# Narrow high passes in the hidden tiles, a reordered LRU and hybrid mixer, an earlier last split in the gated blocks, and the normed activations moved by 64 bytes

## Time and profile before

| | us |
|---|---|
| median of 3 runs (lowest, highest) | 2010.35 (2008.78, 2012.93) |
| the profiled execution, own time | 2012.28 |
| its span | 2010.5 |
| PE busy in the span | 1961.8 (98%) |
| DVE busy | 1373.3 (68%) |
| ACT busy | 916.8 (46%) |

### The profile page before, as it was taken

One profiled execution on the slowest core, in us unless ns is written; L12 is line 12 of the kernel. 1 busy time (PEld: TensorE's weight loads), 2 busy tenths in 40 slices (PEclk: granted clock), 3 DMA queues, 4 the chain that ended last, 5 costly groups with the idle time before them and its releaser, 6 DMA issues.

```text
span 2010.5 us, 27811 instructions
## 1 busy us (share of the span) xinstructions
PE 1961.8 (98%) x11662; PEld 1710.6 (85%) x11662; DVE 1373.3 (68%) x1388; ACT 916.8 (46%) x856; POOL 22.5 (1%) x45
## 2 busy tenths in 40 slices
PE   8999999999999999999999999999999999999998
PEld 7988888797888888888988888878888998998886
DVE  7665866698865787666856685677665556667665
ACT  4445333367434473333435443344445556555443
POOL 0000000000000000000000000000000010000000
PEclk9999999999999999999999999999999999999999
DMA  8444545444554435544644455544546563344552
GB/s 340 169 156 179 188 174 202 176 165 160 217 209 171 162 138 184 205 174 173 223 163 168 162 210 203 178 147 177 194 180 223 191 175 135 119 168 157 188 188 105
DMA packets 31987, 361.69 MB, mean 180 GB/s; under 512 B 3805, under 2 KB 4066, under 8 KB 9746
## 3 DMA queue, kind: packets, MB, share of 16 engines
q1 hardware_dynamic: 28146, 347.49, 47.2%
q0 software_dynamic: 3744, 12.77, 2.7%
HBM read 359.15 MB, written 1.10 MB: 179 GB/s over the span
## 4 chain that ended last, share of the span: by engine, by line
PE 85%; DVE 9%; ACT 4%; issue 1%; DMA 0%; SPq 0%; DVEq 0%; ACTq 0%
PE acc L946 26%; PE bank L1550 10%; PE bank L1637 7%; PE bank L1556 5%; PE bank L836 3%; PE bank L838 3%; PE bank L837 3%; PE bank L1646 3%; DVE w_lo L2523 2%; PE acc L958 1%; PE bank L875 1%; PE bank L876 1%; PE bank L877 1%; PE bank L1181 1%; ACT w_hi L1925 1%
## 5 line engine op out<-in xcount | busy, mean ns | idle before, releaser
L2528 DVE TENSOR_TENSOR w_lo<-raw,w_hi 128x4096 fp32r<-128x4096 f32 (+4 forms) x83 | 310.1, 3737 | 119.1 <-ACT w_hi L1936 119.1
L1936 ACT ACTIVATE w_hi<-raw 128x4096 fp32r<-128x4096 f32 (+4 forms) x91 | 283.5, 3116 | 170.1 <-PE bank L1556 170.1
L1925 ACT ACTIVATE w_hi<-raw 128x2048 fp32r<-128x2048 f32 x166 | 309.6, 1909 | 55.6 <-PE bank L838 38.0
L2523 DVE TENSOR_TENSOR w_lo<-raw,w_hi 128x2048 fp32r<-128x2048 f32 x98 | 220.0, 2287 | 84.6 <-ACT w_hi L1925 84.6
L1550 PE MATMUL bank<-ht_both,w_hi 128*128 128x512 f32 x896 | 213.9, 395 | 0.6 <-DVE mlp_r L2995 0.6
L1550 PEld LDWEIGHTS bank<-ht_both,w_hi 128*128 128x128 f32 x896 | 167.4, 187 | 41.9 <-issue 1.1
L836 PE MATMUL bank<-ht_both,w_hi 128*128 128x256 f32 x704 | 197.9, 281 | 0.0
L838 PE MATMUL bank<-ht_both,w_lo 128*128 128x256 f32 x704 | 196.7, 279 | 0.0
L837 PE MATMUL bank<-ht_both,w_hi 128*128 128x256 f32 x704 | 196.6, 279 | 0.0
L1637 PE MATMUL bank<-ht_both,w_hi 128*128 128x512 f32 x640 | 152.5, 394 | 0.0
L1637 PEld LDWEIGHTS bank<-ht_both,w_hi 128*128 128x128 f32 x640 | 119.6, 187 | 29.1
(11 more groups left out here) (491 smaller groups left out, 3659.6 us busy)
## 6 DMA issues: line engine op xcount, KB each, us to landing
raw<-slabs_in SPq DMA_DIRECT2D x147, 2048.0 KB, 7.7
raw<-slabs_in SPq DMA_DIRECT2D x23, 1024.0 KB, 6.7
raw<-slabs_in SPq DMA_DIRECT2D x12, 512.0 KB, 11.1
g_tab<-gains_in POOLq DMA_DIRECT2D x11, 512.0 KB, 4.2
b_tab<-gains_in POOLq DMA_DIRECT2D x8, 512.0 KB, 4.9
raw<-slabs_in SPq DMA_DIRECT2D x2, 1152.0 KB, 5.6
raw<-slabs_in SPq DMA_DIRECT2D x1, 1280.0 KB, 5.6
a_bias<-bias_rows POOLq DMA_DIRECT2D x8, 128.5 KB, 3.6
```

What stands on the lines that cost most here:

```text
L1925: nc.scalar.activation(w_hi[g % 2][:, c], raw[g % RING][:, c], ACT.Copy)\
L1936: nc.scalar.activation(w_hi[slot][:, 0:w], raw[g % RING][:, 0:w], ACT.Copy).then_inc(hi_ready, 1)
L2523: ins = nc.vector.tensor_tensor(w_lo[ring][:, c], raw[ring][:, c], w_hi[slot][:, c].bitcast(F32), ALU.subtract)
L2528: nc.vector.tensor_tensor(w_lo[ring][:, 0:w], raw[ring][:, 0:w], w_hi[slot][:, 0:w].bitcast(F32), ALU.subtract).then_inc(lo_ready, 1)
```

## The change

In words, part by part:

- In `hidden` of both kinds, bank 0 keeps its wide matmuls; in banks 1 to 3 each wide one becomes two narrow ones with the same weights, the high parts and then the low parts (`high_tile`).
- `ht_both` begins 128 bytes behind the weights' remainder in place of 192.
- In the gated blocks ACT may write the last slab's high part as soon as the last hidden block's high passes are done (`gated_high`), and does so before the last silu. As the low passes may then still read `w_lo` in the ring, SP has a wait of its own before it loads over that slot (`used_up`), and this slab is no part of a loop.
- In the LRU, DVE does `conv_lo` 6 to 9 in a row; ACT does the first pair of sigmoids ahead of `conv_hi` 8 and 9 and its half split behind the fifth pair. PE starts the second slab's high passes with its first half and the high parts alone; the third slab's come before any of its low parts are waited for, both halves interleaved, and DVE makes the activations' low parts before that slab's.
- In the hybrid mixer the squares of tile 0, their root and the scaling move into pair 3 of the dilated heads, the squares of tile 1 and their sum too; the squares go into `gate`, the sums into `sp_t`. DVE then rotates tile 0, scales tile 1, splits a slab and rotates tile 1. The last transposes go to bank 7.

```diff
-        off_w(192)
+        off_w(128)
         ht_both = sb("ht_both", [P, KD, 2, S], F32R)
         ht_hi = ht_both[:, :, 0, :]
         ht_lo = ht_both[:, :, 1, :]
-        off_w(64)
+        off_w(128)
...
-        b_ss = sb("b_ss", [P, TT, 10], F32, er)
-        b_rs = sb("b_rs", [P, TT, 10], F32, er)
+        b_ss = sp_t[:, 2:4, :]
+        b_rs = [sp_t[:, 4 * t, :] for t in range(TT)]
+        b_sq = [gate[:, 6 + 5 * t:11 + 5 * t, :].rearrange("p c (two d) -> p (c two) d", two=2) for t in range(TT)]
...
-            take("bt", i)
+            take("bt", i, slot=7 if i == B_FIRST[-1] else None)
...
-                released[g0 if b == 0 else g0 + 2 * b - 1] = full("ffa", f, 3) if b == 0 else (s1, n1 + b - 1)
+                up = g0 if b == 0 else g0 + 2 * b - 1
+                released[up] = full("ffa", f, 3) if b == 0 else (s1, n1 + b - 1)
+                if b == FFN_B - 1:
+                    used_up[up + RING] = released[up]
+                    released[up] = (gated_high, f + 1)
...
+                    if g in used_up:
+                        sp.wait_ge(*used_up[g])
                     load(g, g % RING, WIDTH[g])
...
+            def high_tile(q, whi, k):
+
+                if q == 0:
+                    return nc.tensor.matmul(bank[q][:, :], whi, ht_both[:, k, :, :].rearrange("p a s -> p (a s)"),
+                                            start=k == 0, stop=False)
+                for i, x in enumerate((ht_hi, ht_lo)):
+                    m = nc.tensor.matmul(bank[q][:, i * S:(i + 1) * S], whi, x[:, k, :], start=k == 0 and i == 0,
+                                         stop=False)
+                return m
...
+            def high_pass(t, g, x, chunks):
+
+                for k in chunks:
+                    for half in range(2):
+                        a = k * D + half * 512
+                        nc.tensor.matmul(acc[t][half][:, :], x[:, k, t * P:(t + 1) * P], w_hi[g % 2][:, a:a + 512],
+                                         start=False, stop=False)
...
-                    high_part(0, ga, ahi, alo, range(kna), first)
-                    high_part(1, ga, ahi, alo, range(a_ahead), first)
...
+                if low_last:
+                    for x in (bhi, blo):
+                        for k in range(knb):
+                            for half in range(2):
+                                a = k * D + half * 512
+                                nc.tensor.matmul(acc[0][half][:, :], x[:, ib + k, 0:P], w_hi[gb % 2][:, a:a + 512],
+                                                 start=False, stop=False)
+                    need(gb)
+                    for half, done_half in enumerate((acc_half, acc_full)):
+                        for k in range(knb):
+                            a = k * D + half * 512
+                            m = nc.tensor.matmul(acc[0][half][:, :], bhi[:, ib + k, 0:P], w_lo[gb % RING][:, a:a + 512],
+                                                 start=False, stop=k == knb - 1)
+                        m.then_inc(done_half, 1)
+                elif b_low is None:
...
-                part(0, gb, bhi, blo, ib, range(knb), last=True, halves=(1,)).then_inc(acc_full, 1)
+                if not low_last:
+                    part(0, gb, bhi, blo, ib, range(knb), last=True, halves=(1,)).then_inc(acc_full, 1)
...
-                    pe.wait_ge(hi_ready, g0 + 8)
+                    g = g0 + 7
+                    pe.wait_ge(piped_half, PIPED[g])
+                    pe.wait_ge(y_hi, 2)
+                    for t in range(TT):
+                        high_pass(t, g, y_hi1, range(2))
+                    pe.wait_ge(hi_ready, g + 1)
                     pe.wait_ge(y_lo, 2)
+                    for t in range(TT):
+                        high_pass(t, g, y_lo1, range(2))
+                        for k in range(2, 4 - t):
+                            for x in (y_hi1, y_lo1):
+                                high_pass(t, g, x, (k,))
...
-                         (g0 + 8, 2, lu_hi, lu_lo, 4, lambda: blocks_ready(2)), a_ahead=3,
+                         (g0 + 8, 2, lu_hi, lu_lo, 4, last_high), a_ahead=3,
...
-                            nc.tensor.matmul(bank[q][:, :], w_hi[g % 2][:, a:a + P],
-                                             ht_both[:, k, :, :].rearrange("p a s -> p (a s)"), start=k == 0, stop=False)
+                            high_tile(q, w_hi[g % 2][:, a:a + P], k)
...
+                            m = high_tile(q, w_hi[g % 2][:, a:a + P], k)
+                    if b == last:
+                        m.then_inc(gated_high, 1)
...
-                for n in range(6, LRU_N):
-                    conv_hi(n)
                 for n in range(LRU_N):
+                    if n == 0:
+                        conv_hi(6)
+                        conv_hi(7)
+                    if n == 1:
+                        conv_hi(8)
+                        conv_hi(9)
...
-                    if n == 2:
+                    if n == 4:
...
+                act.wait_ge(lo_ready, g0 + 2 * FFN_B - 2)
+                split_one()
                 silu(FFN_B - 1)
                 nc.scalar.activation(sp_t[:, 1, 0:1], eps[:, 1:2], ACT.Sqrt)
-                split_one()
...
+                def squares(t):
+                    for s in range(3):
+                        act.wait_ge(*read("b", s, t))
+                    for hd in range(A_H - 2, A_H):
+                        act.wait_ge(*full("as", hd, 1))
+                    nc.scalar.activation(b_sq[t], b_x[:, t, 0:1280].rearrange("p (h d) -> p h d", h=10),
+                                         ACT.Square).then_inc(b_squares, 1)
+
+                def root(t):
+                    act.wait_ge(b_ssq, t + 1)
+                    nc.scalar.activation(b_ss[:, t, :], b_ss[:, t, :], ACT.Sqrt, bias=eps[:, 1:2], scale=1.0 / B_HD)\
+                        .then_inc(b_std, 1)
...
+                    if pr == 3:
+                        squares(0)
+                        root(0)
...
+                    if pr == 3:
+                        squares(1)
...
+                root(1)
...
-                conv_lo(6)
-                conv_lo(7)
+                for n in range(6, LRU_N):
+                    conv_lo(n)
                 dve.wait_ge(piped_half, PIPED[g])
                 low_half(g, 0)
-                conv_lo(8)
-                conv_lo(9)
...
-                split_one()
                 gated_lo(2)
+                split_one()
...
-                    nc.vector.tensor_reduce(b_ss[:, t, :], (b_t, b_o)[t][:, :, :], AX_X, ALU.add).then_inc(b_ssq, 1)
...
+                    nc.vector.tensor_reduce(b_ss[:, t, :], b_sq[t], AX_X, ALU.add).then_inc(b_ssq, 1)
...
+                    if pr == 3:
+                        dve.wait_ge(qk_gain_loaded, 16)
+                        ssq_of(0)
+                        scaled(0)
+                        split_one()
+                        ssq_of(1)
...
+                roped(0)
+                scaled(1)
+                split_one()
+                roped(1)
```

More of the change, by code:

```diff
@@ L354, in program @@
         lo_half = sem("lo_half")
+        gated_high = sem("gated_high")
         ffn_silu = sem("ffn_silu")
@@ L611, in program @@
         released = {}
+        used_up = {}
         used_count = 0
@@ L751, in _ @@
                 while g + RING * turns + RING - 1 < N_SLABS \
+                        and not any(g + v in used_up for v in range(RING * (turns + 1))) \
                         and all(WIDTH[g + RING * turns + u] == WIDTH[g + u] for u in range(RING)):
@@ L1010, in down_end @@
                 b_ready()
-                if b_low is None:
+                if low_last:
[13 more added lines that the diff above has]
+                elif b_low is None:
                     part(0, gb, bhi, blo, ib, range(knb), last=True, halves=(0,)).then_inc(acc_half, 1)
@@ L1312, in lru, with last_high @@
                     branch_low_last(s)
-                def blocks_ready(i):
-                    need(g0 + 6 + i)
-                    pe.wait_ge(y_lo, i + 1)
+                def last_high():
+                    pe.wait_ge(hi_ready, g0 + 9)
+                    pe.wait_ge(y_lo, 3)
                 pe.wait_ge(*read("lin", 5))
@@ L1625, in ffn @@
                 before = [ticket["ffn", f, q][1] - 1 for q in range(4)]
+                last = FFN_B - 1
                 def hidden(b, g, r=0):
@@ L1652, in ready @@
                     pe.wait_ge(ffn_lo_done, r * 2 + (b + FFN_B * f + 1))
-                last = FFN_B - 1
                 n = N_LN + 1 + 2 * f
@@ L2395, in hybrid @@
                         split_one()
-                for t in range(TT):
-                    for s in range(3):
-                        act.wait_ge(*read("b", s, t))
-                    nc.scalar.activation((b_t, b_o)[t][:, :, :], b_x[:, t, 0:1280].rearrange("p (h d) -> p h d", h=10),
-                                         ACT.Square).then_inc(b_squares, 1)
-                for t in range(TT):
-                    act.wait_ge(b_ssq, t + 1)
```

(5 more changed lines are left out.)

51 lines of the change are left out of this document (25 added, 26 removed).

## The result

The changed kernel takes 2026.4 us (median of 4, 2025.29 to 2029.86) against 2010.41 for the kernel before beside it: a ratio of 1.008, 95% interval [1.0065, 1.0095]. It is slower by 16 us, where 13.8 us less were forecast, and it lies outside the range. The profiled span is 2023.5 us against 2010.5.

What follows compares the result with a forecast made beforehand. PE, busy 98% of the span, was taken as the bound. Savings of 7.5 + 0 + 2.5 + 1.4 + 2.4 = 13.8 us gave 1998.5 from the profiled 2012.28, or 1996.5 us for the median; 8-in-10 range 1984 to 2009.

Steps and rivals of the forecast that it cites:

- Step 2: Moving `ht_both` from 192 to 128 bytes: narrow matmuls' mean price taken as unchanged, 0 us; bounds -9.5 and +24 us.
- Rival D: 128 bytes is a bad distance for narrow matmuls streaming `ht_both`: +24 us, 2020 us; chance 0.12.
- Step 1: Hidden blocks, banks 1 to 3: 1152 wide matmuls become cheap narrow pairs, -7.5 us; bounds -7.5 and +2.6.
- Step 3: Gated ends: last slab's high part written earlier removes PE's 1.25 us wait twice, -2.5 us; bounds 1.5 and 2.8.
- Step 4: LRU reordering: norm 0.9 us earlier plus 0.5 allowed for the chain in front, -1.4 us; bounds 0 and 3.
- Step 5: Hybrid mixer: PE's waits for tile 1's rotation and ACT's copies both go, -2.4 us; bounds 0 and 2.5.
- C: Rival: removed waits in gated ends, LRU and hybrid mixer return as others, 4.5 of 6.3 us lost; 2001 us, chance 0.14.

Runs made afterwards that it cites:

- e1: The changed kernel with the activations' tile back at 192 bytes; 1997.6 us, 0.992 of the kernel before.
- e2: The kernel before with the activations' tile moved from 192 to 128 bytes and nothing else; 2028.49 us, 1.0077 of the kernel before.
- e5: e1 with a pad ahead of `w_lo` as well, so that weights and activations move together by 192 bytes; 1996.67 us, 0.9934 of the kernel before.
- e3: The kernel before, tile at 192 bytes, with only the high passes of banks 1 to 3 split into narrow ones; 2003.81 us, 0.9954 of the kernel before.
- e8: e1 with bank 0's high passes narrow as well, so no bank wide; 2013.2 us, 1.0013 of the kernel before.
- e4: The changed kernel with the tile at 192 bytes and all four banks wide, leaving gated ends, LRU and hybrid mixer; 2005.85 us, 0.9966 of the kernel before.
- e10: e1 with only the first two of bank 0's eight wide matmuls left wide, the other six split; 1995.74 us, 0.9921 of the kernel before.

## Why the prediction was wrong

**Step 2 failed: the tile's move was taken as 0 and costs 15.6 us alone, 28.8 with the rest** (2026.4 - 1997.6; 32 by the two ratios, each against the kernel before beside it). Three things in that step were wrong, and two of them could be read from the trace of before.

First, "midway between" 64 and 192: the price does not run steadily with the distance. 128 and 160 both have 118.75 in the block of the table, above 64 and 192, and 192 stands alone.

Second, the row at 64 was read as a mixture, "dear on average between 276 and 281". The same line by single durations (ns minimum/median/maximum), in the kernel before:

```profile
L837 PE MATMUL bank<-ht_both,w_hi x704: 276/281/283, 24.2 to 1718.5; 128*128 128x256 f32 x176
...
L837 PE MATMUL bank<-ob_lo,w_hi x64: 279/279/279, 1769.7 to 1791.9; 128*128 128x256 f32 x64
```

L837 with `ht_both` has a mean of 279 out of 276 and 281. `ob_lo` has 279 for each of its 64, so there are no cheap ones among them. By the starts its price is the dear one: from 1769.66 to 1791.92 us are 63 steps of three, 117.8 ns. With that, no row of before but those at 192 showed a cheap narrow matmul, and three distances (0, 64, 192) of which two are dear give no ground for a midpoint.

Third, the upper bound of +24 us was too low. It had 5,300 matmuls rising from 113.2 to 117.7, while 128 has 118.6 to 118.7, and 120.0 in some projections. The trace of before held a price above 117.7: the `lu_hi` and `lu_lo` matmuls at 0 bytes, 47 starts from 434.67 to 440.17 us, take 119.6 ns each. The step called them "dear or above" and then reckoned with 117.7. Rival D was the right one, with 0.12: its place, its mechanism and its test (durations of 281 in the new passes, L837 towards 281 or above) are what the profile shows, and its price was some 6 us too small (2020 against 2026.4). Its point of decision, a rise of the mean of 1.9 ns, is passed by L881 with 5 and by L846 to L848 with 2 to 3 over e1's.

The Trainium skill, page "TensorE: Matmul & The Clock Gate", step "DRAIN" of "Step-by-step: what each phase is for", says that loaded and streamed operands are read through independent ports. e2 and e5 disagree with what follows from it for the time: the same instructions cost 15.6 us more when 64 bytes are put between the two tiles' remainders, and nothing when both move.

**Step 1** (-7.5) is right: e3 is 0.46% faster, 9.3 us, with 7.5 within its interval (0.29 to 0.63%, or 5.8 to 12.7 us), and by the spans 7.7 (2010.5 - 2002.8). Its 2,304 have a median of 276, for the reason given, bank 0's wide ones ahead of them. That reason carried more than I knew: e8 shows that without them a block behind a way down is dear. At 128 the same split costs: two narrow ones are 237.5 against 232.5, which is 5.8 us over 1,152 (an estimate, as no run makes the split alone there). By the Trainium skill, same page, section "Back-to-back issue gap", the split would cost an estimated 2.9 us. e3 contradicts that in sign at 192; at 128 the sign is the page's.

**Steps 3, 4 and 5** (-2.5, -1.4, -2.4, together -6.3) are right in sum: e4 is 0.34% faster, 6.8 us, interval 4.4 to 9.3. Singly they are not. I set e4's PE beside that of the kernel before, matmul by matmul, and read by how much its lead grows at each place: 1.5 us at each of the two gated ends, 3.1 together; 0.9 in the LRU; 1.6 and 1.2 at the two waits of the hybrid mixer. Steps 3 and 5 were under-sized, by 0.6 and 0.4, and step 4 was over-sized by 0.5, so part of the agreement of the sum is luck. The whole span of e4 is 9.3 us shorter; the rest is the start and the net of projections and first tiles whose narrow streams ran at one price in one trace and at the other price in the other.

Step 3: L1016's two waits are gone from every kernel that has the change. ACT and DVE at the end of the first gated block in the changed kernel, as the earlier trace rows:

```profile
1523.77 1.92 ACT L1988 ACTIVATE w_hi<-raw 128x2048 fp32r<-128x2048 f32 x1 [5.20 <-PE bank L881]
```

```profile
1528.87 2.28 DVE L2595 TENSOR_TENSOR w_lo<-raw,w_hi 128x2048 fp32r<-128x2048 f32 x1
```

ACT now writes the last slab's high part as soon as PE's high passes end, 5.1 us ahead of DVE's split. DVE begins its split with no idle time in front, where it waited 1.49 before, as the step said.

Step 4: e4's DVE at the end of the LRU, as the earlier trace rows:

```profile
486.58 0.69 DVE L2901 TENSOR_TENSOR lu_lo<-lru_u,lu_hi 128x512 fp32r<-128x512 f32 x1 [0.69 <-ACT lu_hi L2204]
487.18 2.28 DVE L2595 TENSOR_TENSOR w_lo<-raw,w_hi 128x2048 fp32r<-128x2048 f32 x1
490.30 0.69 DVE L2652 SCALAR_TENSOR_TENSOR h<-h,acc 128x512 f32<-128x512 f32 x1 [0.83 <-PE acc L1048]
```

The swap of split and activations is there. The norm begins at 490.30 in place of 492.23, but e4 had entered the LRU 1.0 us ahead already. Its first matmul:

```profile
399.38 0.36 PE L1303 MATMUL bank<-ht_both,w_hi 128*128 128x256 f32 x1 [0.67 <-DVE ht_both L2631]
```

and that of the kernel before:

```profile
400.40 0.36 PE L1262 MATMUL bank<-ht_both,w_hi 128*128 128x256 f32 x1 [0.67 <-DVE ht_both L2564]
```

From there to the norm are 90.92 us against 91.83, 0.9 us less, and e1 has 90.90. That is the 0.9 that the step derived for the swap; the 0.5 that it allowed for the chain in front did not come. The waits did come back in part, as C had it: PE now waits for `lu_lo` before the first slab, 2.3 us in e4, which is the early arrival at the scan that the step named, and still before the last slab, 1.2. Together with 0.2 at L986 the LRU's waits are 3.7 us in e4 against 5.0, where a fall of about 3 was forecast.

Step 5: both waits are gone, and in the changed kernel DVE's idle time ahead of pair 3's split has shrunk from the 9.28 us of the earlier trace rows to 3.53; nothing new waits in that stage.

Without step 2 the forecast of 1996.5 stands 1.1 us from e1's 1997.6. Part of that nearness is luck: the kernel before stood at 2012.86 beside e1 and at 2010.35 in the forecast, so the gain was 15.3 where 13.8 was forecast. The failed step had bounds of -9.5 and +24, more than all others together, and yet the chance of 0.82 for faster was that of the steps that I could cost; a step with such an upper bound and no row at its own distance deserved far more than the 0.12 of D.

## What to carry to other kernels

- Where PE is busy throughout, the remainder of 256 bytes between the tile that is loaded and the tile that is streamed is a parameter worth several microseconds; move one tile, measure, and treat it as unknown between measured points. Count how many matmuls stream the tile before and after a change: here a split of 1,152 wide matmuls nearly doubled what a bad distance costs (28.8 us in place of 15.6).
- Read prices from the starts. A mean duration between two known values need not be a mixture, and one and the same duration can stand for two prices: 279 was 117.8 ns at 64 bytes, and 281 was 117.7 at 192 and 120.0 at 128.
- Before you credit a gain to a stage, measure from the stage's own start in both traces. Here 1.0 of 1.9 us had been won before the stage began.
- A stream of narrow matmuls keeps the price that it enters with; here two wide ones ahead of 92 narrow ones were worth 4 ns for each of these.

## What the runs showed of the hardware

- A 128x256 fp32r matmul behind its like costs, where the granted clock is a 9 throughout, by the distance of the two tiles: 119.6 to 120.0 ns at 0 bytes, 113.3 or 117.9 at 64, 118.6 to 118.7 or 120.0 at 128, 118.7 or (in five blocks and some projections) 117.3 at 160, 113.3 to 113.5 or 117.7 at 192, 118.1 to 118.4 at 224. A 128x512 one costs 232.5 to 233 at 128 and 192, and 226.6 at 0. Of these distances 0 is best for wide ones and worst for the blocks' narrow ones.
- At 64, 128, 160 and 192 bytes a stream has one of two prices. At 64 and 192 it keeps it for 80 matmuls and more (128 in e8's gated blocks), until a wait or matmuls of another shape. Which one it takes depends on what runs ahead: at 192 two wide matmuls of the same tile behind a way down make it cheap (e10), none leaves a block behind a way down dear (e8).
- Moving both tiles together by 192 bytes changes nothing that can be measured here (e5: 1996.67 against 1997.6).

Why the distance acts, and why streams behind a wait fall on either side, stays open; the runs show when, not how.
